# First x block on ScalarE's queue, turned and split in halves; GpSimd's loads behind its clears

## The reference

```python
def reference(x, pre_norm_g, w_in, mlstm_i_bias, mlstm_f_bias, conv_w, conv_b,
              attn_out_g, mlstm_out_g, w_out, post_norm_g):
    ...
    for l in range(DEPTH):
        h = rms_norm(x, pre_norm_g[l])
        proj = jnp.einsum('bsd,dc->bsc', h, w_in[l])
        aq, ak, av, az, mq, mk, mv, mo, mz, mi, mf = split_columns(proj)
        ya = moba_attention(partial_rope(att_heads(aq), pos), partial_rope(att_heads(ak), pos), att_heads(av))
        ya = rms_norm(ya, attn_out_g[l]) * jax.nn.silu(az)
        qk = jax.nn.silu(causal_depthwise_conv(jnp.concatenate([mq, mk], axis=-1), conv_w[l], conv_b[l]))
        ...
        hm = mlstm_chunkwise(...)
        ...
        y = jnp.einsum('bsc,cd->bsd', jnp.concatenate([ya, ym], axis=-1), w_out[l])
        x = x + rms_norm(y, post_norm_g[l])
    return x
```

## Time and profile before

| | |
|---|---|
| median of 3 runs | 317.78 us (317.5 to 318.87) |
| span of the profiled execution, first to last instruction | 316.2 us (its time with what lies around the span is not given apart) |
| TensorE busy | 98% |
| VectorE, ScalarE, GpSimd busy | 71%, 52%, 30% |
| chain that ended last | 93% on TensorE, 2% DMA, 3% issue |
| mean DMA rate | 121 GB/s |

### The profile page before, as it was taken

One profiled execution on the slowest core, in us unless ns is written; L12 is line 12 of the kernel. 1 busy time (PEld: TensorE's weight loads), 2 busy tenths in 40 slices (PEclk: granted clock), 3 DMA queues, 4 the chain that ended last, 5 costly groups with the idle time before them and its releaser, 6 DMA issues.

```text
span 316.2 us, 4992 instructions
## 1 busy us (share of the span) xinstructions
PE 309.4 (98%) x1599; PEld 256.4 (81%) x1599; DVE 225.4 (71%) x508; ACT 165.2 (52%) x336; POOL 95.9 (30%) x118
## 2 busy tenths in 40 slices
PE   8999999999999999999999999999999999999992
PEld 4888888888888888888888888778888888888882
DVE  2544999748998699968998568964577766856534
ACT  3548857287345324663157563384556876353301
POOL 8201006056350213002320025592711984000000
PEclk9999999999999999999999999999999999999999
DMA  7941553956725486645864332210220473310111
GB/s 222 323 99 38 153 149 93 170 163 150 134 68 146 134 158 205 188 124 122 180 227 151 102 90 77 73 66 31 67 68 0 125 200 145 133 68 0 68 66 67
DMA packets 29081, 38.30 MB, mean 121 GB/s; under 512 B 3624, under 2 KB 15184, under 8 KB 29056
## 3 DMA queue, kind: packets, MB, share of 16 engines
q1 hardware_dynamic: 27424, 34.51, 36.2%
q0 software_dynamic: 1472, 3.34, 7.0%
q10 hardware_dynamic: 160, 0.14, 0.1%
HBM read 33.68 MB, written 4.29 MB: 120 GB/s over the span
## 4 chain that ended last, share of the span: by engine, by line
PE 93%; issue 3%; DMA 2%; DVE 0%; DVEq 0%; SPq 0%; ACT 0%; POOLq 0%; POOL 0%; ACTq 0%
PE bank L1476 24%; PE bank L1478 24%; PE bank L1477 24%; PE bank L1814 3%; PE bank L1524 3%; PE bank L1758 3%; PE bank L1779 3%; PE bank L1612 2%; DMA farena<-in_x 2%; PE bank L1708 1%; PE bank L1505 1%; PE bank L1769 1%; PE bank L1613 1%; PE bank L1552 1%; PE bank L1551 1%
## 5 line engine op out<-in xcount | busy, mean ns | idle before, releaser
L778 ACT ACTIVATE w_hi<-w_raw 128x512 fp32r<-128x512 f32 x71 | 43.7, 626 | 63.2 <-PE bank L1478 51.1
L1476 PE MATMUL bank<-w_hi,xT_hi 128*128 128x512 f32 (+1 forms) x180 | 72.5, 403 | 0.0
L1478 PE MATMUL bank<-w_hi,xT_lo 128*128 128x512 f32 (+1 forms) x180 | 69.8, 388 | 0.0
L1477 PE MATMUL bank<-w_lo,xT_hi 128*128 128x512 f32 (+1 forms) x180 | 69.3, 385 | 0.0
L1043 DVE TENSOR_TENSOR w_lo<-w_raw,w_hi 128x512 fp32r<-128x512 f32 x64 | 45.5, 721 | 11.1 <-ACT w_hi L778 11.0
L1476 PE MATMUL bank<-xT_hi,w_hi 128*128 128x512 f32 x128 | 50.8, 397 | 0.0
L1478 PE MATMUL bank<-xT_hi,w_lo 128*128 128x512 f32 x128 | 50.1, 392 | 0.0
L1477 PE MATMUL bank<-xT_lo,w_hi 128*128 128x512 f32 x128 | 50.0, 390 | 0.0
L1478 PEld LDWEIGHTS bank<-w_hi,xT_lo 128*128 128x128 f32 x180 | 33.8, 188 | 7.2
L1476 PEld LDWEIGHTS bank<-w_hi,xT_hi 128*128 128x128 f32 x180 | 33.9, 188 | 5.8 <-issue 0.4
L1477 PEld LDWEIGHTS bank<-w_lo,xT_hi 128*128 128x128 f32 x180 | 34.0, 189 | 5.5
(11 more groups left out here) (211 smaller groups left out, 581.8 us busy)
## 6 DMA issues: line engine op xcount, KB each, us to landing
w_raw<-in_w_in SPq DMA_DIRECT2D x72, 256.0 KB, 2.9
w_raw<-in_w_out SPq DMA_DIRECT2D x16, 256.0 KB, 2.7
kq_rows<-stage SPq DMA_DIRECT2D x8, 256.0 KB
gy<-kq_rows SPq DMA_DIRECT2D x8, 256.0 KB, 3.5
gy<-in_x SPq DMA_DIRECT2D x4, 512.0 KB, 5.4
out_y<-gy SPq DMA_DIRECT2D x7, 256.0 KB, 2.1
farena<-in_x SPq DMA_DIRECT2D x4, 256.0 KB, 5.3
farena<-in_x SPq DMA_DIRECT2D x2, 512.0 KB, 7.5
```

Of the source, the lines that this page charges most:

```text
L778: a.activation(hi, raw, ACT.Copy).then_inc(w_hi_done, 1)
L1476: pe.matmul(o, hi, m_hi, start=start, stop=False)
L1477: pe.matmul(o, hi, m_lo, start=False, stop=False)
L1478: return pe.matmul(o, lo, m_hi, start=False, stop=stop)
```

## The change

The first x block is issued by ScalarE ahead of `prow`, so that SyncE's queue begins with w slot 0. The block's work in three engines is done in halves of 256 tokens: two transposes to a bank (half 0 in bank 4, half 1 in bank 5), an activation, a VectorE instruction for each. The semaphores of these steps count one more (`x_parts(k)` is k + 2), and the turn of block 1 now waits for both low halves, since one lay in its bank. In slot 0 the order is hi times hi by halves, x_lo times w_hi by halves, then the turn of block 1, then x_hi times w_lo. The dummy products are 6 of 512 columns ahead of the turns (5 and a half before) and 2 of 256 columns behind them (3 of 512 before). GpSimd's six loads into `prow2` stand behind its clears and masks.

```diff
@@ SyncE
-                if n in X_BEFORE:
+                if X_BEFORE.get(n):
                     load_x(X_BEFORE[n])
@@ GpSimd: this block moves up, ahead of the six loads into prow2
+            g.wait_ge(w_hi_done, 1)
+            g.memset(wg[:].bitcast(F32), 0.0).then_inc(wg_clear, 1)
...
+            g.memset(mv[:, :, MV + MD:].bitcast(F32), 0.0).then_inc(mv_ones, 1)
+
             g.wait_ge(par2_clear, 1)
             g.dma_start(prow2[0:4, :], rows_of(attn_g)).then_inc(par2_in, 16)
...
@@ ScalarE
+            def x_hi_half(q):
+                half = slice(q * HALF_SEQ, (q + 1) * HALF_SEQ)
+                a.wait_ge(xt_ps, q + 1)
+                a.wait_ge(par_done, 1)
+                a.activation(xT_hi[:, 0, half], bank[4 + q][:, half], ACT.Copy, scale=pcol[:, R_PRE:R_PRE + 1])\
+                    .then_inc(xt_hi, 1)
+
             def x_hi(k):
-                a.wait_ge(xt_ps, k + 1)
+                a.wait_ge(xt_ps, x_parts(k))
...
+            a.dma_start(x_sb[:, :, 0:P], x.rearrange("b s d -> (b s) d")[:, 0:P].rearrange("(t p) d -> p t d", p=P))\
+                .then_inc(x_in[0], 16)
             a.dma_start(prow[:], pre_g.rearrange("o (c p) -> (o c) p", p=P)).then_inc(par_in, 16)
             a.activation(ssx[:, 0:1], ones, ACT.Copy)
-            x_hi(0)
+            x_hi_half(0)
+            x_hi_half(1)
@@ VectorE
+            def x_low_half(q):
+                half = slice(q * HALF_SEQ, (q + 1) * HALF_SEQ)
+                v.wait_ge(xt_hi, q + 1)
+                v.scalar_tensor_tensor(out=xT_lo[:, 0, half], in0=bank[4 + q][:, half], scalar=pcol[:, R_PRE:R_PRE + 1],
+                                       in1=f32(xT_hi[:, 0, half]), op0=ALU.mult, op1=ALU.subtract).then_inc(xt_lo, 1)
...
-            x_low(0)
+            x_low_half(0)
+            x_low_half(1)
             cut(0)
@@ TensorE
-            keep_busy(5)
-            keep_busy(1, AW // 2)
+            keep_busy(6)
...
+            def turn_x_half(q):
+                pe.wait_ge(x_in[0], 16)
+                for t in (2 * q, 2 * q + 1):
+                    mm = pe.transpose(bank[4 + q][:, t * P:(t + 1) * P], x_sb[:, t, 0:P], ident[:])
+                mm.then_inc(xt_ps, 1)
+
             def turn_x(k):
                 pe.wait_ge(x_in[X_OF[k]], 16)
-                if k >= 2:
-                    pe.wait_ge(xt_lo, k - 1)
+                pe.wait_ge(xt_lo, max(2, x_parts(k - 2)))
...
-                pe.wait_ge(xt_hi, k + 1)
                 pe.wait_ge(w_hi_done, k + 1)
-                mv_terms(k, 0)
-                turn_x(k + 1)
-                pe.wait_ge(xt_lo, k + 1)
-                mv_terms(k, 1)
+                if k == 0:
+                    for term, done in ((0, xt_hi), (1, xt_lo)):
+                        for q in range(2):
+                            pe.wait_ge(done, q + 1)
+                            mv_terms(k, term, (2 * q, 2 * q + 1))
+                    turn_x(k + 1)
+                else:
+                    pe.wait_ge(xt_hi, x_parts(k))
+                    mv_terms(k, 0)
+                    turn_x(k + 1)
+                    pe.wait_ge(xt_lo, x_parts(k))
+                    mv_terms(k, 1)
                 low_done(pe, k)
                 mv_terms(k, 2).then_inc(w_used, 1)
...
-            turn_x(0)
-            keep_busy(3)
+            turn_x_half(0)
+            turn_x_half(1)
+            keep_busy(2, AW // 2)
```

More of the change, by code:

```diff
@@ L66, with x_parts @@
 WIDE_UNTIL = 4
+HALF_SEQ = SEQ // 2
+def x_parts(k):
+    return k + 2
 FIRST_ON_POOL = S_MO
@@ L600, in _ @@
                             pattern=[[-1, P]], channel_multiplier=1).then_inc(ident_done, 1)
[L601 to L609, removed]
             g.wait_ge(w_hi_done, 1)
@@ L631, in _ @@
             g.memset(mv[:, :, MV + MD:].bitcast(F32), 0.0).then_inc(mv_ones, 1)
+            g.wait_ge(par2_clear, 1)
+            g.dma_start(prow2[0:4, :], rows_of(attn_g)).then_inc(par2_in, 16)
+            g.dma_start(prow2[4:8, :], rows_of(mlstm_g)).then_inc(par2_in, 16)
+            g.dma_start(prow2[8:16, :], rows_of(conv_b)).then_inc(par2_in, 16)
+            g.dma_start(prow2[16:48, :], conv_w.rearrange("o j (c p) -> (o j c) p", p=P)).then_inc(par2_in, 16)
+            for q, bias in enumerate((i_bias, f_bias)):
+                row = R_BIAS - R_AG + q
+                g.dma_start(prow2[row:row + 1, :].rearrange("o (j h) -> o j h", h=MH),
+                            bias.unsqueeze(1).to_broadcast([1, P // MH, MH])).then_inc(par2_in, 16)
             g.dma_start(rope_sb[:], rope.rearrange("(t p) c -> p t c", p=P)).then_inc(rope_in, 16)
@@ L1057, in x_low @@
             def x_low(k):
-                v.wait_ge(xt_hi, k + 1)
+                v.wait_ge(xt_hi, x_parts(k))
                 v.scalar_tensor_tensor(out=xT_lo[:, k, :], in0=bank[4 + k % 2][:],
@@ L1517, in by_slot, with mv_terms @@
                 mm.then_inc(w_used, 1)
-            def mv_terms(k, term):
+            def mv_terms(k, term, tiles=range(NT)):
                 (x_hi, x_lo), (wk_hi, wk_lo) = (xT_hi, xT_lo), w_part(k)
                 xs, ws = ((x_hi, wk_hi), (x_lo, wk_hi), (x_hi, wk_lo))[term]
-                for t in range(NT):
+                for t in tiles:
                     mm = pe.matmul(bank[t][:], xs[:, k, t * P:(t + 1) * P], ws, start=k + term == 0, stop=False)
@@ L1548, in gate_rows_of @@
                 pe.wait_ge(wg_done, 2)
-                pe.wait_ge(xt_lo, NK)
+                pe.wait_ge(xt_lo, x_parts(NK - 1))
                 for k in range(NK):
```

## The result

The changed kernel takes 320.68 us (median of 6 runs, 320.39 to 322.01), the kernel before 318.05 (6 runs, 317.5 to 319.08). The ratio is 1.0087, interval 1.0069 to 1.0106: 2.6 us slower, where 0.5 us faster was forecast and the range ended at 318.6.

A forecast was written before the change was run, and what follows sets the result against it. TensorE, busy 98% of the span, was taken as the bound, so only its early idle time could be gained. The terms -0.1 and -0.38 made -0.5 us against 317.78, giving 317.3, range 316.5 to 318.6.

The forecast's parts named there:

- P: Start of slot 1's first product, 9.20 before, forecast near 8.7; the change was to be worth what it moves.
- Part 1: Loads' issuers at the start: x block 0 on ScalarE's queue lands at 4.0, between 3.6 and 4.8.
- S: Start of the first real product, 5.52 before; forecast 5.4, bounds 4.95 and 6.2.
- The rule of the Trainium skill: DMA engines take turns between queues packet by packet, bringing x block 0's landing near the upper bound, 4.8.
- Part 2: First x block in halves: 0.47 each on ScalarE, 0.49 on VectorE; first real product 0.1 us sooner.
- Part 3: Slot 0's order: 0.44 stall goes, -0.38 us, provided ScalarE has cut w slot 1 before rounding x block 1.
- rival (c): Slot 1's weights come late: slot 1 starts at 9.0, total 317.6; its chance lies within the forecast's 0.55.
- Part 4: GpSimd's loads behind its clears: cost 0, cover 8 us; x block 1 and w slot 1 possibly sooner.
- (a): First x block late, at 4.8: slot 1 starts at 9.5, +0.3, total 318.1; chance 0.15.
- (b): TensorE's clock rises later because of idle gaps: five slot 0 products slow, +1.0, total 318.3; chance 0.2.

The follow-up runs named there:

- e1: Kernel before with only the loads' issuers changed (x block 0 by ScalarE ahead of the gain row): 320.81 us, ratio 1.0088.
- e5: Changed kernel with w slot 0 and then x block 0 both on SyncE's queue: 319.3 us, ratio 1.0026.
- e11: Kernel before with only the new order of slot 0 (turn of x block 1 behind the eighth product): 318.09 us, ratio 1.0003.
- e12: Kernel of e11 with four dummies behind the first turn, not three: 318.10 us, ratio 1.0016.
- e7: Changed kernel with the gain row issued ahead of x block 0 on ScalarE's queue: 320.51 us, ratio 1.0076.
- e8: Changed kernel with SyncE's first issue held until the identity is written: 319.42 us, ratio 1.0042.
- e10: Kernel before with two dummies of 256 columns behind the first turn in place of three of 512: 319.84 us, ratio 1.0061.
- e6: Changed kernel with SyncE's queue beginning with x block 1, w slot 0 behind it: 319.56 us, ratio 1.0039.
- e9: Kernel of e2 with three dummies of 512 columns behind the turn in place of two of 256: 318.15 us, ratio 1.0009.
- e4: Changed kernel with 12 dummy products ahead of the gain row's turn, not 6: 319.35 us, ratio 1.0041.
- e2: Changed kernel with x block 0 back heading SyncE's queue and GpSimd's loads back ahead of its clears: 318.34 us, ratio 1.0016.
- e3: Kernel before with only GpSimd's six loads moved behind its clears: 318.23 us, ratio 1.0003.

## Why the prediction was wrong

**What bounds the kernel: right, nearly.** What moves P moves the end: in seven of the thirteen profiles the distances from the kernel before at P and at the end agree within 0.15 us (e1 to e5, e11, e12; from -0.33 to 3.51 at P). In the other six the end is later than P says, though, by 0.2 to 0.5 in e7, e8, e10 and the changed kernel, 0.9 in e6 and 1.2 in e9. The step near 70 us is the larger part of it in four of them, the wait told at the end of this text that of e9. The prediction had named this as what would make it wrong as a whole; it adds 0.4 us to the changed kernel's profile, but doesn't make the loss.

**Part 1 is the step that failed.** x block 0 was put at 4.0 with 4.8 as the end of the range; it landed at 5.1 (5.2 to 5.7 in e4, e1 and e7). S was put at 5.4, 6.2 at the latest, and came at 7.25. Two things were missing: not only w slot 0 moves beside x but x block 1 too, since both were now issued before 1.7 (by 4.5 us SyncE's queue has moved 0.35 MB, more than the slot's 256 KB); and with w slot 0 and x block 0 begun together, all queues together move little more than half of what they did before, until 3.5. The bound had been taken from a time at which x led and the rate was full. The gain row was put 0.05 behind x; it came 0.5 behind, at 5.60, and was the last thing waited for. The rule of the Trainium skill that the prediction set against this part ("DMA: Bandwidth & Descriptors") had the right sign; the upper bound, 4.8, which the prediction gave it as its price, was too low. That the weights don't decide S held in the changed kernel, but not where x block 0 stayed in its place (e2 and e9, above).

**Part 2 was right in its sizes.** The halves cost 0.47 each on ScalarE (0.90 for the two with their overlap) and 0.48 on VectorE, as worked out; S came 1.35 us after the turn began (5.90 to 7.25; 1.15 forecast, the transposes being at the slow clock). That they bring anything was not seen: where x was early, the weights decided S. "The shorter dummies fill idle time", costed at nothing without a reason, was the second error: e10 prices it at 1.9 us in the kernel before, e2 and e9 at 0.2 beside the halves and the new order.

**Part 3 was right in its mechanism, not in its worth.** The stall went; P - S is 3.34 to 3.42 in each profile in which the clock was up (e4, e5, e8, e9, e11) against the 3.3 worked out. Its condition on slot 1's weights was met: rival (c) did not happen. In the changed kernel the slow clock covered it. But the 0.38 us that it was to bring did not come even alone, in e11: the profile has 0.33 at P and 0.2 at the end, the runs nothing.

**Part 4 was right**: 1.0003 alone, x block 1 no sooner.

**The rivals.** (a), x late, had the mechanism but not the size, and (b), the late rise, came together with it and was not an alternative to it: late loads alone bring it (e1), shorter dummies alone bring it too (e10), and the change has both. The gap that (b) named was 0.6 us by the forecast of x and 2.17 in fact. Their prices were +0.3 and, for five slow products, +1.0; the profile has eight and part of four more. The two together account for about the 2.6 us. e4 takes the slow products out and leaves 1.3 (ratio 1.0041): the late loads, and 0.3 by which its dummies overshoot. Giving (a) and (b) separate chances, with a forecast between, was the error in the chances: slower by over 0.5% had 0.06.

**What stays open.** That the dummies' number and place change how many real products are slow is shown (e4, e10). That it is the idle gap which delays the rise is argued only: e5 and e8 have gaps and fast products, e3 and e12 have slow products with no gap ahead of S. Whether a gap ahead of the turn and one behind it weigh the same was not tried apart: e4 closes the one, e9 and e10 the other. Nor is it shown why the first weight rows are slow.

## What to carry to other kernels

A load moved to a second queue "at the same moment" loses its place at the head of the first: what was behind it now runs beside it, and a small row behind it waits as well. Where dummy work fills the time until TensorE's clock rises, its length is part of the schedule: before something that it waits for is moved, or a dummy is shortened because it "fills idle time", price the whole first slot at the slow level. Look at the spread of all runs as well, since one profile shows one moment of the rise. And rivals that are consequences of each other belong in one case with one sum.

## What the runs showed of the hardware that was not expected

The granted clock's column doesn't show the level at the start. The window of the changed kernel from 7.50 to 8.50 us, in the midst of products 0.43 apart, says 1.00, like one behind the rise:

```profile
7.50:8.50 1.00, 1.00 (x3) 0.81 (x4) 1.00 (x3) 0.55 (x2) 1.00 (x4) 1.00 1.16 331
12.70:13.70 1.00, 1.00 (x5) 0.81 (x5) 1.00 (x2) 0.40 (x1) 1.00 (x3) 1.00 0.74 241
```

Here only the distance of equal products tells it. And one VectorE instruction can take twice its time: in e9's profile the gating of one tile took 1.84 us, in the kernel before 0.88; TensorE then waited 1.1 us, and the 0.3 us won at the head had become 0.9 lost. Why that instruction took so long was not found.

```profile
252.19 1.84 DVE L1344 SCALAR_TENSOR_TENSOR gy<-stage,gy 128x512 f32<-128x512 f32 x1 [0.74 <-ACT stage L773]
```

```profile
252.24 0.88 DVE L1320 SCALAR_TENSOR_TENSOR gy<-stage,gy 128x512 f32<-128x512 f32 x1 [0.47 <-ACT stage L764]
```
